# Attention pipeline one step deeper: a fourth score buffer, transposes three steps and values four steps behind the scores

## What is computed

```python
def _sb_block(q, k, v, bias, q_pos, k_pos):
    z = jnp.einsum('bhqd,bhkd->bhqk', q, k) * (SB_HEAD_DIM ** -0.5) + bias[None, :, None, None]
    mask = k_pos[None, :] < q_pos[:, None]
    log_beta = jax.nn.log_sigmoid(z)
    log_rest = jnp.where(mask, jax.nn.log_sigmoid(-z), 0.0)
    tail = lax.cumsum(log_rest, axis=3, reverse=True) - log_rest
    A = jnp.where(mask, jnp.exp(log_beta + tail), 0.0)
    return jnp.einsum('bhqk,bhkd->bhqd', A, v)
```

## Time and profile before

| | |
|---|---|
| median of 3 runs | 2318.68 us (2316.85 to 2319.75) |
| the profiled execution (its span) | 2321.0 us |
| busy TensorE, its weight loads | 2147.9 us (93%), 2005.6 us (86%) |
| busy VectorE, ScalarE, GpSimd | 46%, 26%, 25% |
| mean granted clock of TensorE | 0.952 of 2.4 GHz |

### The profile page before, as it was taken

One profiled execution on the slowest core, in us unless ns is written; L12 is line 12 of the kernel. 1 busy time (PEld: TensorE's weight loads), 2 busy tenths in 40 slices (PEclk: granted clock), 3 DMA queues, 4 the chain that ended last, 5 costly groups with the idle time before them and its releaser, 6 DMA issues.

```text
span 2321.0 us, 31837 instructions
## 1 busy us (share of the span) xinstructions
PE 2147.9 (93%) x12704; PEld 2005.6 (86%) x12704; DVE 1079.1 (46%) x1169; ACT 604.1 (26%) x760; POOL 589.4 (25%) x392
## 2 busy tenths in 40 slices
PE   6999999999999999999978889789999999999994
PEld 5887898878988899878968889579999999999993
DVE  4277555775367663765534652452222223222235
ACT  3234412343223432345123421220100101001011
POOL 1221112211111211211112232343232333323322
PEclk9997999989998999989989999899999999999997
DMA  4220204102131121312144333201111120111132
GB/s 141 57 93 28 58 28 127 52 19 67 47 114 37 48 56 58 101 39 58 38 159 149 111 102 120 102 14 55 32 50 41 41 59 29 52 45 36 54 106 79
DMA packets 203987, 156.89 MB, mean 68 GB/s; under 512 B 15730, under 2 KB 188402, under 8 KB 203890
## 3 DMA queue, kind: packets, MB, share of 16 engines
q1 hardware_dynamic: 201698, 146.89, 20.4%
q10 hardware_dynamic: 2192, 8.65, 1.0%
HBM read 120.16 MB, written 35.35 MB: 67 GB/s over the span
## 4 chain that ended last, share of the span: by engine, by line
PE 85%; DVE 7%; ACT 5%; issue 1%; DMA 1%; POOL 0%; POOLq 0%; SPq 0%; DVEq 0%; ACTq 0%
PE psum L364 69%; PE psum L601 4%; PE psum L621 3%; PE psum L666 3%; PE psum L612 2%; PE psum L569 1%; DVE hid L1482 1%; PE psum L648 1%; DVE mix L1467 1%; PE psum L630 1%; DVE arena L1170 1%; DVE x_again L1461 0%; DMA conv_full<-c_d 0%; DVE hid_lo L1484 0%; DVE mix L1457 0%
## 5 line engine op out<-in xcount | busy, mean ns | idle before, releaser
L364 PE MATMUL psum<-h_hi,w_hi 128*128 128x352 f32 x2400 | 541.7, 334 | 37.1 <-DVE h_lo L1174 10.9
L364 PE MATMUL psum<-h_hi,w_lo 128*128 128x352 f32 x2400 | 525.7, 327 | 0.0
L364 PE MATMUL psum<-h_lo,w_hi 128*128 128x352 f32 x2400 | 525.6, 328 | 0.0
L364 PEld LDWEIGHTS psum<-h_hi,w_hi 128*128 128x128 f32 x2400 | 412.1, 193 | 75.9 <-issue 53.1
L364 PEld LDWEIGHTS psum<-h_hi,w_lo 128*128 128x128 f32 x2400 | 419.8, 191 | 0.0
L364 PEld LDWEIGHTS psum<-h_lo,w_hi 128*128 128x128 f32 x2400 | 416.3, 192 | 0.0
L341 POOL CAST w_hi<-w_raw 128x1024 fp32r<-128x1024 f32 x60 | 71.9, 1198 | 913.7 <-PE psum L364 895.1
L354 POOL CAST w_hi<-w_raw 128x512 fp32r<-128x512 f32 (+1 forms) x128 | 96.5, 754 | 732.5 <-PE psum L364 643.3
L356 POOL TENSOR_TENSOR w_lo<-w_raw,w_hi 128x512 fp32r<-128x512 f32 (+1 forms) x128 | 229.7, 1794 | 10.3
L1140 ACT ACTIVATE hid<-psum 128x1056 f32<-128x1056 f32 x32 | 33.7, 1054 | 583.1 <-PE psum L364 583.1
L364 PE MATMUL psum<-hid_hi,w_hi 128*128 128x352 f32 x768 | 166.4, 325 | 10.8 <-DVE hid_lo L1484 10.8
(11 more groups left out here) (226 smaller groups left out, 2459.8 us busy)
## 6 DMA issues: line engine op xcount, KB each, us to landing
w_raw<-in_w_in SPq DMA_DIRECT2D x60, 512.0 KB, 4.0
w_raw<-in_w_ff SPq DMA_DIRECT2D x32, 512.0 KB, 4.0
w_raw<-in_w_ff SPq DMA_DIRECT2D x64, 256.0 KB, 2.7
g_d<-gate_logits SPq DMA_DIRECT2D x24, 528.0 KB, 2.7
gates<-g_d SPq DMA_DIRECT2D x24, 528.0 KB, 3.6
arena<-in_xT SPq DMA_DIRECT2D x8, 528.0 KB, 7.0
x_again<-in_xT SPq DMA_DIRECT2D x1, 4224.0 KB, 13.8
x_d<-x_again ACTq DMA_DIRECT2D x8, 528.0 KB, 2.7
```

Of the source, the lines that this page charges most:

```text
L364: mm = pe.matmul(ps[:, b0 + g, 0:GW], w[:, slot, k, :], x[:, k, g * GW:(g + 1) * GW], start=(k == 0 and w is wh and x is xh), stop=(k == k ...
```

## The change

A fourth score buffer `z_more` (128 x 1024 f32) is put behind the other tensors of the group stage, and all three engines take `zb[i % 4]` for `zb[i % 3]`. TensorE runs `turn_a(s - 3)` and `values(s - 4)` in step `s`, in 20 steps; ScalarE copies item s - 4 in step `s`, in 21 steps, and the output blocks one step later. Halves, samples and scores stay in their steps, so steps 10, 13, 18 and 19 have no half.

```diff
+        z_more = sb("z_more", [P, 1024], F32, s2)[:, :]
...
-            zb = [A(o, 1024) for o in A_Z]
+            zb = [A(o, 1024) for o in A_Z] + [z_more]
...
-                    mm = pe.transpose(banks(5, 1024)[:, kb * P:(kb + 1) * P], zb[i % 3][:, kb * P:(kb + 1) * P], ident)
+                    mm = pe.transpose(banks(5, 1024)[:, kb * P:(kb + 1) * P], zb[i % 4][:, kb * P:(kb + 1) * P], ident)
...
-                for s in range(19):
+                for s in range(20):
                     if s < 16:
                         scores(p, s)
                     if s in A_STEPS:
                         half(A_STEPS.index(s) // 2, A_STEPS.index(s) % 2)
                     if s == 3:
                         v_staged.wait(pe, p, 1)
-                    if s >= 3:
-                        values(p, s - 3)
-                    if s == 2:
-                        v_staged.wait(pe, p, 1)
-                    if 2 <= s < 18:
-                        turn_a(p, s - 2)
+                    if s >= 4:
+                        values(p, s - 4)
+                    if 3 <= s < 19:
+                        turn_a(p, s - 3)
...
-                for s in range(20):
-                    i = s - 3
+                for s in range(21):
+                    i = s - 4
...
-                    if s >= 5 and s % 2 == 1:
-                        qb = (s - 5) // 2
+                    if s >= 6 and s % 2 == 0:
+                        qb = (s - 6) // 2
...
-                        if s >= 3:
-                            t_done.wait(act, p, s - 2)
+                        if s >= 4:
+                            t_done.wait(act, p, s - 3)
```

More of the change, by code:

```diff
@@ L943, in group @@
                         z_ready.wait(act, p, s + 1)
-                        if s >= 3:
-                            t_done.wait(act, p, s - 2)
+                        if s >= 4:
+                            t_done.wait(act, p, s - 3)
                         n = P * (s // 2 + 1)
-                        act.activation(zb[s % 3][:, 0:n], banks(3, n), IDN, bias=sbp[:, s % 2:s % 2 + 1])\
+                        act.activation(zb[s % 4][:, 0:n], banks(3, n), IDN, bias=sbp[:, s % 2:s % 2 + 1])\
                             .then_inc(z_read.sem, 1)
@@ L957, in group @@
                         n = P * ((s - 2) // 2 + 1)
-                        z = zb[(s - 2) % 3][:, 0:n]
+                        z = zb[(s - 2) % 4][:, 0:n]
                         arg_ready.wait(act, p, s - 1)
@@ L1236, in group @@
                         n = P * (qb + 1)
-                        z, l = zb[s % 3][:, 0:n], lb[s % 2][:, 0:n]
+                        z, l = zb[s % 4][:, 0:n], lb[s % 2][:, 0:n]
                         z_read.wait(dve, p, s + 1)
@@ L1251, in group @@
                         n = P * ((s - 1) // 2 + 1)
-                        z, l = zb[(s - 1) % 3][:, 0:n], lb[(s - 1) % 2][:, 0:n]
+                        z, l = zb[(s - 1) % 4][:, 0:n], lb[(s - 1) % 2][:, 0:n]
                         ln_ready.wait(dve, p, s)
```

## The result

The changed kernel takes 2293.77 us in the median of four runs (2290.09 to 2296.4), beside 2317.76 for the kernel before in the same comparison: a ratio of 0.9886, 95% interval 0.9865 to 0.9906, or 24.0 us less. The forecast was 2291.3. The profiled execution is one of those runs, the fastest (2290.09 us, span 2288.3); against the span of before, 2321.0, it is 32.7 us shorter. The profiled execution of before has a longer span than any of the four runs of that kernel took. So this pair of profiles makes the gain look larger than the runs do.

A forecast was written before the change was run, and what follows sets the result against it. TensorE, 85% of the chain that ended last, bounds the kernel through stalls and low clock; 6.0 + 8.8 + 12.5 + 5.3 - 5.2 = 27.4 us off 2318.7 gives 2291.3 us, range 2282 to 2311.

The forecast's parts named there:

- Steps 10 and 13, the stalls: TensorE's stalls of 1.49 and 2.20 us a group go, saving 6.0 and 8.8 us.
- the spares of 0.9 and 1.0 us: Margins before `values(9)` in step 13 and `scores(14)` would wait for ScalarE's copies; no new wait was counted.
- The end of the steps: In step 18 `values(14)` waits for a bare copy, 1.3 us a group, costing 5.2 us; clock stays up.
- Rival 1: Clock falls at the end of the steps behind stalls of 1.3 and 1.11 us; 2310 us, chance 0.20.
- The clock after step 13: Without the stall, groups 0, 1 and 3 keep full clock there: 12.5 us less, bounds 0 and 13.8.
- The clock around step 10: The drop stays but ends earlier, at most 5.4 us a group: 5.3 us less, bounds 0 and 10.7.
- The sum: 6.0 + 8.8 + 12.5 + 5.3 - 5.2 = 27.4 us less, from 2318.7 to 2291.3 us.
- Rival 2: Clock falls in and after step 13 anyway, from samples, missing halves or narrow work; 2309 us, chance 0.10.
- Rival 3: Waits only move: `values(9)`, `scores(14)` or `scores(11)` wait for ScalarE's copies; 2324 us in full, chance 0.07.
- rival 4: Slower: the end of the steps at low clock for 18 us, 8.5 us a group; 2325 us, chance 0.08.

The follow-up runs named there:

- the kernel with the filled end: Changed kernel with the last half unit cut up over steps 17 to 19 and that unit copied out last by ScalarE: 2283.21 us, ratio 0.9846.
- the halves early: Kernel before (three buffers, lags of two and three) with the 16 half units in steps 0 to 15: 2304.64 us, ratio 0.9944.

## Why the prediction was right, point by point

- **Steps 10 and 13, the stalls.** 6.0 and 8.8 us were to go, and both waits are gone. No new wait came up in steps 10 to 14: the spares of 0.9 and 1.0 us held. The buffer alone left both waits standing, the lag alone lost time, and each wait put back brought its stall back. So the lag removes them, and it needs the buffer.
- **The end of the steps.** 1.3 us a group was forecast, 1.28 is measured (5.2 us for L939), and the old 1.11 stayed. Filling both with matmuls gave 10.1 us, close to their sum of 9.7. One thing that the profile was to show is not there: the stretch from `values(13)` to `turn9(iT)` is not 1.3 us longer but shorter, 258.03 - 247.56 = 10.47 us in group 0 for 267.22 - 252.26 = 14.96, because the half of step 17 (6 us) now stands ahead of `values(13)`. The cost of the stall does not hang on that.
- **Rival 1, the clock at the end.** It did not come: 1.00 over 245 to 268 us, through both stalls, and the same in the other three groups. The rule of the page "TensorE: Matmul & The Clock Gate" of the Trainium skill (section "Part 4: PE-mode transpose") was weighed there; this case's trace does not agree that such a stretch, part of it transposes, loses the clock. A stretch of transposes alone was not run.
- **The clock after step 13.** Forecast 12.5 us. The changed kernel's profile has full clock there, as said. But the size came from one execution with the low clock in three groups of four; a second profile of the same order, that of the buffer alone, had it in one, 11 x 0.47 = 5.2 us where the first gave 13.8. For that execution the term was over-sized; for the median the runs do not settle it.
- **The clock around step 10.** Forecast 5.3 us, bounds 0 and 10.7 (4 x 2.71 is 10.8). The mechanism held: the drop stays, since it follows the narrow matmuls, and it gets shorter. The size did not: in group 0 it is 7 us shorter where at most 5 were forecast. By length times missing clock the four stretches are 29.0 us before and 13.8 after, 15.2 less. Of these 3.0 are half of the stalls' own 6.0 us, counted there already, so some 12 us are left, or 11 if scaled as the step 13 term was (4.71 for 5.17): in these two profiles the upper bound was a little too low. I had assumed that the clock would need as long to come back as in group 0, which had one of the shorter stretches of before. The runs' times are less clear: putting the stall back cost 12.2 us, 6.6 of them clock, which lies inside the bounds; how large the term is in the median stays open. And the length varies with no stall at all, from 7 us to 18 (group 0 of the kernel with the filled end).
- **The sum.** Idle time changed by 14.8 - 5.2 = 9.6 us, as forecast. The other 14.4 of the 24.0 us are clock, by subtraction, where 17.8 were forecast. So the idle terms were right one by one. The clock's were right only together: step 13 was taken from a profile that showed much of it, step 10 was sized too low, and the two errors go against each other. That the sum came out within 2.5 us (2291.3 and 2293.8) is in part luck.
- **Rivals 2, 3 and 4.** Rival 2 is refuted for step 13 by the profile after. One of the causes it names, the narrow work, is at work in step 10: the narrow matmuls bring the clock down there, shown by spreading them. Rival 3 has no row that speaks for it (no wait at L602 or L622 in steps 11 to 14), nor has rival 4 (the end at 1.00).

## What to carry to other kernels

In a queue written out by hand, look for steps in which no independent work covers the other engines' latency. There a deeper lag removes the stall. Moving the cover is the other way: here it gave 14.4 of the 24.0 us without a fourth buffer, and paid with stalls at the end. A deeper pipeline pays one more bare hand-over where it drains; fill that with pieces of work held back for it, as here with nine matmuls for each of the two. Read clock losses as something that one profile only samples; idle terms could be added up here, clock terms not safely.

## What the runs showed of the hardware

- TensorE busy with narrow matmuls is not enough to keep the clock: around 32 matmuls of 8 columns, which take 3.7 us at full clock, it was at about half for 4 to 18 us, with a stall behind them or without, and even with a dense half unit behind the next scores (8 us at 0.57). The same matmuls in four lots of eight, with nine dense ones between the lots, leave it at 1.00.
- Stalls of 2.2 to 2.4 us were followed by the low clock in some groups and not in others of the same execution; stalls of 1.28 and 1.11 us, 3 us apart, never were in the changed kernel's profile. With stalls of 1.01 and 1.24 us shortly ahead of these two (the halves early) it fell in two groups of four, at the stall of 1.28.
- The same program at the same place was at the low clock for 7 us in one execution and 14 in another.
